# Sampled sequences' cached values in a decoder step: which operand is stationary on TensorE

## What is computed

```
for window, dil in ((128, 1), (512, 4), (2048, 16)):      # three dilation groups
    kg, vg = k_all[:, idx], v_all[:, idx]                  # 128 cached rows each, and the own one
    s = einsum('nqhe,nqjhe->nqhj', q, kg) * 64**-0.5 - slopes * (dil * j)
    p = exp(s - logsumexp(s))
    o = einsum('nqhj,nqjhe->nqhe', p, vg)                  # the values: what is changed
# the three outputs are merged with weights proportional to their softmax denominators
```

## Time and profile before

| | |
|---|---|
| median of 3 runs | 2173.68 us (2171.97 to 2174.41) |
| the profiled execution | 2172.77 us |
| its span, first to last instruction | 2171.1 us |
| granted TensorE clock, mean | 0.984 of full speed |
| TensorE (PE) busy | 2099.8 us, 97% |
| VectorE (DVE) busy | 1175.1 us, 54% |
| ScalarE (ACT) busy | 874.9 us, 40% |
| GpSimd (POOL) busy | 197.5 us, 9% |
| HBM read | 366.86 MB, 171 GB/s over the span |

### The profile page before, as it was taken

How to read it: one execution, slowest core, us unless ns; L and a number is a source line. 1 busy time by engine, 2 the same in 40 slices (tenths; PEclk the granted TensorE clock), 3 DMA queues, 4 the chain that set the end, 5 groups by cost and what they waited for, 6 DMA issues and landing times.

```text
span 2171.1 us, 44928 instructions
## 1 busy us (share of the span) xinstructions
PE 2099.8 (97%) x18500; PEld 2066.8 (95%) x18500; DVE 1175.1 (54%) x1203; ACT 874.9 (40%) x981; POOL 197.5 (9%) x175
## 2 busy tenths in 40 slices
PE   6999999999999999999997879999999999999997
PEld 5999999999999999999995779999999999999997
DVE  5555555555454555669866545555555555544432
ACT  4444444444443443434315424444444444433432
POOL 3000000000000000024202841000000000000000
PEclk9999999999999999999997989999999999999998
DMA  5655555555555566577861025555655555555652
GB/s 160 184 184 176 183 183 178 181 182 181 173 186 177 174 185 196 155 220 227 255 198 39 9 90 175 186 178 183 183 176 182 183 180 179 182 174 186 194 170 93
DMA packets 359390, 373.38 MB, mean 172 GB/s; under 512 B 13397, under 2 KB 351865, under 8 KB 359206
## 3 DMA queue, kind: packets, MB, share of 16 engines
q1 hardware_dynamic: 349280, 348.17, 51.3%
q0 software_dynamic: 6288, 17.51, 3.2%
q10 hardware_dynamic: 3742, 6.52, 0.9%
HBM read 366.86 MB, written 5.32 MB: 171 GB/s over the span
## 4 chain that ended last, share of the span: by engine, by line
PE 93%; DVE 4%; ACT 1%; DMA 1%; issue 1%; ACTq 0%; POOL 0%; POOLq 0%; SPq 0%; DVEq 0%
PE ps L316 29%; PE ps L318 29%; PE ps L317 29%; DVE wL L303 1%; PE ps L1077 1%; PE ps L1418 1%; DMA raw<-in_w_in_dram 1%; DVE xL L350 0%; PE ps L1664 0%; PE ps L1667 0%; PE ps L1675 0%; DMA vrowa<-in_rwkv_mu_dram 0%; PE ps L1706 0%; PE ps L1691 0%; PE ps L1409 0%
## 5 line engine op out<-in xcount | busy, mean ns | idle before, releaser
L303 DVE TENSOR_TENSOR wL<-raw,wH 128x1024 fp32r<-128x1024 f32 (+1 forms) x676 | 828.0, 1231 | 864.5 <-ACT wH L297 864.1
L297 ACT ACTIVATE wH<-raw 128x1024 fp32r<-128x1024 f32 (+1 forms) x676 | 700.0, 1038 | 1013.8 <-PE ps L318 947.8
L316 PE MATMUL ps<-xH,wH 128*128 128x264 f32 x3616 | 1031.7, 285 | 12.3 <-DVE wL L303 12.2
L318 PE MATMUL ps<-xH,wL 128*128 128x264 f32 x3616 | 1029.5, 285 | 0.0
L317 PE MATMUL ps<-xL,wH 128*128 128x264 f32 x3616 | 1029.4, 285 | 0.0
L316 PEld LDWEIGHTS ps<-xH,wH 128*128 128x128 f32 x3616 | 683.6, 189 | 14.2 <-issue 13.4
L318 PEld LDWEIGHTS ps<-xH,wL 128*128 128x128 f32 x3616 | 683.3, 189 | 0.0
L317 PEld LDWEIGHTS ps<-xL,wH 128*128 128x128 f32 x3616 | 682.8, 189 | 0.2
L316 PE MATMUL ps<-hH,wH 128*128 128x264 f32 x1408 | 402.8, 286 | 0.0
L318 PE MATMUL ps<-hH,wL 128*128 128x264 f32 x1408 | 401.9, 285 | 0.0
L317 PE MATMUL ps<-hL,wH 128*128 128x264 f32 x1408 | 401.7, 285 | 0.0
(11 more groups left out here) (355 smaller groups left out, 1131.5 us busy)
## 6 DMA issues: line engine op xcount, KB each, us to landing
raw<-in_ffn_w_gate_dram SPq DMA_DIRECT2D x176, 512.0 KB, 3.5
raw<-in_ffn_w_up_dram SPq DMA_DIRECT2D x176, 512.0 KB, 3.5
raw<-in_ffn_w_down_dram SPq DMA_DIRECT2D x128, 512.0 KB, 3.4
raw<-in_w_in_dram SPq DMA_DIRECT2D x100, 512.0 KB, 4.8
raw<-in_ffn_w_down_dram SPq DMA_DIRECT2D x64, 384.0 KB, 2.9
raw<-in_w_out_dram SPq DMA_DIRECT2D x32, 512.0 KB, 3.6
kb<-in_cache_swa_k_dram POOLq DMA_DIRECT2D x24, 256.0 KB, 6.5
vb<-in_cache_swa_v_dram ACTq DMA_DIRECT2D x24, 256.0 KB, 5.6
```

Source lines behind the costliest of these rows:

```text
L297: nc.scalar.activation(wH[:, k % RING, 0:nk, :], raw[:, k % RING, 0:nk, :], ACT.Copy).then_inc(S("head_made"), 1)
L303: nc.vector.tensor_tensor(wL[:, k % RING, 0:nk, :], raw[:, k % RING, 0:nk, :], wH[:, k % RING, 0:nk, :].bitcast(F32), ALU.subtract).then_i ...
L316: nc.tensor.matmul(out, wH[:, k % RING, q, cols], high, start=a, stop=False)
L318: last = nc.tensor.matmul(out, wL[:, k % RING, q, cols], high, start=False, stop=b)
```

## The change

The roles of the operands are swapped. The probabilities of one sequence and group, 32 columns of `pS` (8 heads, and 24 columns of zeros), are the stationary operand; the 128 x 512 cached values move. The three sequences of a triple write to PSUM partitions 0, 32 and 64, three column groups of 32; the third triple has two sequences. ScalarE copies the bank to `vm`, and TensorE picks for each head pair the rows of its two heads with columns of the identity as the moving operand (`pe_collect_values`), which puts the result back to features on partitions, in bank 5. `pS` is larger and is cleared by POOL. `values_used` now counts triples, and the loads of a triple wait for one signal instead of three.

```diff
-    pS = at("pS", [P, 3, 2, 32], F32, A0 + 37376)
+    pS = at("pS", [P, 3, NB, 32], F32, A0 + 32512)
+    vm = at("vm", [96, 2, 512], F32, A0)
...
-            23: [lambda: act_load_values(act, (3, 4, 5))],
-            24: [lambda: act_load_values(act, (6, 7))],
+            23: [lambda: act_load_values(act, (3, 4, 5)), lambda: act_sample_values(act, 0)],
+            24: [lambda: act_load_values(act, (6, 7)), lambda: act_sample_values(act, 1)],
...
-            22: [lambda: pe_sample_values(pe, (0, 1, 2))],
-            23: [lambda: pe_sample_values(pe, (3, 4, 5))],
-            24: [lambda: pe_sample_values(pe, (6, 7))],
+            22: [lambda: pe_sample_values(pe, 0)],
+            23: [lambda: pe_collect_values(pe, 0), lambda: pe_sample_values(pe, 1)],
+            24: [lambda: pe_collect_values(pe, 1), lambda: pe_sample_values(pe, 2)],
...
                             ).then_inc(S("conv_turned"), 1)
+        pe_collect_values(pe, 2)
...
-    def pe_sample_values(pe, seqs):
-        pe.wait_ge(S("sample_columns"), 1)
-        for b in seqs:
-            pe.wait_ge(S(f"values_in{b % 3}"), 48 * (b // 3 + 1))
-            for j in range(4):
-                m = 4 * b + j
-                for g in range(3):
-                    last = nc.tensor.matmul(
-                        ps[:, 4, 2 * m:2 * m + P].rearrange("p (n a) -> p n a", a=2), vb[:, b % 3, g, j * P:j * P + P],
-                        pS[:, g, :, m].unsqueeze(1).broadcast_to([P, C, 2]), start=g == 0, stop=g == 2)
-            last.then_inc(S("values_used"), 1)
+    TRIPLES = ((0, 1, 2), (3, 4, 5), (6, 7))
+
+    def pe_sample_values(pe, n):
+
+        pe.wait_ge(S("sample_columns"), 2)
+        for b in TRIPLES[n]:
+            pe.wait_ge(S(f"values_in{b % 3}"), 48 * (n + 1))
+        if n:
+            pe.wait_ge(S("values_out"), n)
+        for g in range(3):
+            for b in TRIPLES[n]:
+                rows = slice(b % 3 * 32, b % 3 * 32 + 32)
+                last = nc.tensor.matmul(ps[rows, 4, :], pS[:, g, b, :], vb[:, b % 3, g, :], start=g == 0, stop=g == 2)
+        last.then_inc(S("values_used"), 1)
+
+    def pe_collect_values(pe, n):
+
+        k = len(TRIPLES[n])
+        pe.wait_ge(S("values_out"), n + 1)
+        for j in range(4):
+            pick = ident[0:32 * k, 0:32 * k].rearrange("p (b r) -> p b r", r=32)[:, :, j:j + 5:4]
+            out = ps[:, 5, 64:128].rearrange("p (b j a) -> p b j a", j=4, a=2)[:, 3 * n:3 * n + k, j, :]
+            last = nc.tensor.matmul(out, vm[0:32 * k, n % 2, j * P:j * P + P], pick, start=True, stop=True)
+        last.then_inc(S("values_collected"), 1)
+
+    def act_sample_values(act, n):
+        k = len(TRIPLES[n])
+        act.wait_ge(S("prompt_kv_out"), 32)
+        act.wait_ge(S("values_used"), n + 1)
+        if n == 2:
+            act.wait_ge(S("values_collected"), 1)
+        nc.scalar.activation(vm[0:32 * k, n % 2, :], ps[0:32 * k, 4, :], ACT.Copy).then_inc(S("values_out"), 1)
...
-                act.wait_ge(S("values_used"), b - 2)
+                act.wait_ge(S("values_used"), b // 3)
...
-        act.wait_ge(S("values_used"), NB)
-        act.wait_ge(S("prompt_kv_out"), 32)
+        act.wait_ge(S("values_collected"), 3)
...
-        nc.vector.tensor_copy(pS[:].rearrange("p g a m -> p (g a m)"), ps[:, 7, 0:192]
-                              ).then_inc(S("sample_columns"), 1)
+        dve.wait_ge(S("columns_cleared"), 1)
+        turned = ps[:, 7, 0:192].rearrange("p (g a b j) -> p g a b j", g=3, a=2, j=4)
+        for a in range(2):
+            nc.vector.tensor_copy(pS[:, :, :, 4 * a:4 * a + 4], turned[:, :, a]).then_inc(S("sample_columns"), 1)
...
-        dve.wait_ge(S("values_used"), NB)
+        dve.wait_ge(S("values_collected"), 3)
...
-            v.tensor_tensor(oo[f, :], ps[f, 4, 0:64].rearrange("p (m a) -> p m a", a=2)[:, :, a], osf[f, :], ALU.add
+            v.tensor_tensor(oo[f, :], ps[f, 5, 64:128].rearrange("p (m a) -> p m a", a=2)[:, :, a], osf[f, :], ALU.add
...
+        pool.wait_ge(S("key_products"), NB)
+        nc.gpsimd.memset(pS[:], 0.0).then_inc(S("columns_cleared"), 1)
         for n, a in ((2, 0), (3, 2)):
...
-        pool.wait_ge(S("values_used"), NB)
+        pool.wait_ge(S("values_used"), 3)
...
     def act_gates(act):
+        act_sample_values(act, 2)
         act.wait_ge(S("mixed"), 2)
```

## The result

The changed kernel took 2159.44 us (median of 4 runs, 2157.71 to 2162.93) where the kernel before took 2174.05 us in the same set (4 runs, 2171.97 to 2175.61): the ratio is 0.9939 [0.9925, 0.9953], 14.6 us less. The direction was right. The same kernel was run in two more sets later. Its 15 runs together have a median of 2161.6 us (2157.6 to 2164.4), against 2173.3 us for the 88 runs of the kernel before that stood beside all sets (2169.5 to 2176.6). So the gain is nearer 11.7 us than 14.6, and the first four runs happened to lie low. What follows explains most of both numbers, and says what stays open.

The account below looks back on a forecast made before the run. TensorE bounds the kernel, 93% of the span. Bursts and collections win 10.65 us, the hop gives back 1.15: 9.5 us off 2172.77 is 2163.3, plus 0.9 for the median, 2164.2 us; range 2161.0 to 2168.6.

Parts of the forecast that it names:

- A burst: TensorE's sampled-value matmuls between dense products, stages 22 to 24: about 3.0 us each, where 7.95, 7.95 and 5.35 us stood.
- The change ahead of it I count the same: Switch of matmul shape on TensorE ahead of the value matmuls: taken as 0.2 us, like the switch behind them.
- A collection: TensorE's four matmuls, eight records, that pick each head's rows: 0.9 us, the upper end of 0.5 to 0.9 us.
- The hop: From the third burst's end to L1394, through ScalarE's copy, Tanh, Sigmoid and Square: 4.8 us for 3.66, 1.15 us given back.
- reaction 0.46 us: Delay from the third burst's end to the start of ScalarE's copy, taken from POOL's delay behind the turn.
- Loads of stage 23: Nine value DMAs landing at 1113.9 to 1115.2, wanted by TensorE at 1114.7: slack 0 to 0.5 us, taken as 0.
- The stretch ahead of the first burst: TensorE before stage 22's values: only POOL's memset could cost there, up to 0.5 us over a late weight chunk, taken as 0.
- The width: Forecast's own range, 2161.5 to 2166.5: clock and run spread 1.7 us, collections 0.4 less each, late loads 0.5, POOL 0.5.
- Rival 1: In the three bursts, column groups start in program order: 3.8 us lost, 2168.0 us; chance 0.10.
- Rival 2: Stage 23's cached values land late for the second burst, 4.0 us behind their need: 2168.2 us; chance 0.08.
- Rival 3: In the three bursts, groups don't overlap and each change drains the array: 16.6 us lost, 2180.8 us, slower; chance 0.04.
- Rival 4: Clock fall moving to the front of L1394: 1.1 us lost, or 1.6 us won if it stays up; no chance given.

Follow-up runs that it names:

- e3: Changed kernel with ScalarE's third copy moved behind Tanh and Sigmoid: 2160.72 us, ratio 0.9948 to the kernel before.
- e9: Changed kernel with ScalarE's third copy behind Tanh and Sigmoid and the first nine value loads spread over stages 20 to 22: 2159.26 us, ratio 0.9936.
- e10: e9 with two of VectorE's three rounds of convolution taps moved from stage 21 to stage 22: 2160.24 us, ratio 0.9942 to the kernel before.
- e1: Kernel before with POOL's memset alone, ahead of its stores, and VectorE's wait for it: 2170.68 us, ratio 0.9989.
- e12: Kernel before with the memset alone, placed behind POOL's stores and table loads: 2173.55 us, ratio 0.9999.
- e7: Changed kernel with all sequences of a triple in one column group, values not kept apart: 2175.96 us, ratio 1.0016 to the kernel before.
- e2: Changed kernel with POOL's memset moved behind the loads of the tables: 2164.34 us, ratio 0.9962 to the kernel before.
- e0: Changed kernel run again without any edit: 2161.21 us, ratio 0.9945 to the kernel before.
- e11: Changed kernel run once more without any edit, in another set: 2163.53 us, ratio 0.9949 to the kernel before.
- e5: Kernel before with POOL's three lora table loads moved behind its wait for the turned probabilities: 2172.94 us, ratio 0.9997.
- e13: Kernel before with the memset ahead of the stores and the first nine value loads spread over stages 20 to 22: 2171.91 us, ratio 0.9995.

## Why the prediction was right or wrong

**Direction and main mechanism: right.** The bursts overlap in three column groups. The forecast had 10.65 - 1.15 = 9.5 us for the bursts and the hop; measured are 11.33 - 0.65 = 10.7 us.

- *A burst, 3.0 us expected.* Measured 2.71 us. The 2.60 us of three matmuls in a row are right; the change of shape costs 0.1 us in all, not 0.2 us on each side. The three bursts with their collections beat the forecast by 0.29, 0.31 and 0.11 us. The step "The change ahead of it I count the same" was mis-sized.
- *A collection, 0.9 us expected.* Measured 1112.83 - 1111.95 = 0.88 us, 0.110 us a record. The upper end was the right choice.
- *The hop, +1.15 us expected.* Measured +0.65. Copy (0.59), Tanh to Sigmoid (1131.49 to 1133.64, 2.15 us) and Square (1.51) came as priced. The "reaction 0.46 us" was taken from POOL; ScalarE's copy started 0.16 us behind the turn. That the Square and not `lnwr` or the collection sets L1420's start was right, and e3 shows it.
- *Loads of stage 23, slack 0 to 0.5 us.* No wait in the changed kernel: the landing took 4.7 to 6.3 us, and the burst wanted them at 1112.83. The slack was small, as said. In e9 and e10 the second burst was due as long after the first one (15.3 us), but the loads took up to 8.2 and 8.9 us to land, and TensorE waited 1.7 and 2.6 us.
- *The stretch ahead of the first burst.* This is the step that failed: for it the sum had only POOL's memset, "up to 0.5 us of that could reach TensorE over a late weight chunk, I take 0". The place was right, the size and the sign were not. In the first pair of profiles the late chunk of stage 21 lands 27.2 us behind the start of `pe_values` for 29.4, the wait is 1.0 us for 3.1, and the stretch is 3.5 us shorter. How much of that is the memset's doing stays open. Its 0.74 us (expected near 0.7) stand ahead of the stores and loads. In the kernel before it was worth 2.4 us (e1), and nothing behind the loads (e12). In e7 nothing of a gain is seen, between the changed kernel and e2 the times don't decide, and the wait was 1.0 to 3.4 us with the memset in the same place. So a good part of the 3.5 us was the luck of one execution.
- *The width.* The range counted 1.7 us for "the clock and the spread of runs". One kernel's profiles differ by 3.8 us in the stretch ahead of the first burst alone, and 15 runs by 6.8 us, so a median of four can lie 2 us beside that of fifteen, as it did.

Together: 9.5 us forecast, 1.2 us more from the bursts and the hop, makes 10.7, and this part repeats in every profile of the changed kernel. About 1 us more leads to the 11.7 us of all runs; it may be the memset, but it is no larger than what the runs can't tell apart. 2161.6 us is inside the range. The other 3 us of the first set go with the wait and the clock ahead of stage 22 and with the clock behind L1420, which differ between executions of one kernel. Below 2161.0 us the range had nothing, since POOL's part was only allowed to cost and the spread between executions was put too small.

**The rivals.** Rival 1, a strict order of the column groups, is false: a burst would have taken at least 4.3 us. The Trainium skill (TensorE: Matmul & The Clock Gate, Part 3, The mechanism) has the rule that it came from, that matmuls start and end strictly in program order. The trace does not agree with it for the two records of these matmuls in column groups: the first records of the three groups start 7 ns apart, all within 0.02 us, and the second record of the first matmul only 0.45 us behind its first. Rival 2, late values, is false here and true in e9 and e10. Rival 3, no overlap, is what e7 builds: 2175.96 us, slower than before, as its sign said. The forecast for it, 2180.8 us, had 3.6 us for changes of group, which e7 doesn't make; without them it is 2177.2 us, 1.2 us above e7. Rival 4, the clock, was width, and real: in the first profile the 12 records of L1420 took 4.14 us beside 4.28, in e0 4.52 us, and in e11 5.36 us at a granted clock of 0.52. That is the 5.4 us at half speed that the prediction priced, 1.1 us lost, and it came in one of three profiles of the same kernel.

**Still open.** Whether the memset does anything in the changed kernel, and why a delay of about 0.9 us on POOL's queue should let the chunk of stage 21 land earlier in the kernel before. The value loads compete with it (landing at 25.6 us with them spread, 29.4 without), the tables' loads don't show it in the times (e5), and the stores weren't tried alone. In e13 the stores started 0.3 us behind `pe_values`, no later than the 0.5 to 0.7 us of the kernels without a memset, and 1.6 us in e1; so the memset doesn't always delay them against TensorE. Nor was the wait ahead of stage 22 seen in more than one profile of each experiment, so its mean for each kernel is known only through the times (the unedited kernels have two and three profiles).

## What to carry to other kernels

Small matmuls with few stationary columns belong side by side in column groups, the groups innermost in the order of issue; check in the trace that their first records start together, because in one group the same count was slower than the code replaced. A small instruction on a queue that issues DMAs moves their issue in time: give it a range with a gain in it as well as a loss, as e1 had one. And where a stretch of the trace holds a wait with a half-speed stretch behind it, look at a second profile of the same kernel before putting its length into a sum.

## What the runs showed of the hardware that was not expected

- Three column groups of 32 with all 128 rows and 512 columns ran at 2.9 times the rate of one group, 2.71 us against 7.84 us for nine matmuls. The Trainium skill gives 2.38 for three tiles at 512 columns (TensorE: Matmul & The Clock Gate, Part 3, Measured speedup vs the span model); the trace is nearer to the full three.
- A memset of 0.74 us on POOL, added to the kernel before and used by nobody, went with a faster run: 2170.68 us, 0.9989 [0.998, 0.9998]; behind the table loads it did nothing, 0.9999 [0.999, 1.0008]. The same memset in the changed kernel showed no clear effect.
- One weight chunk landed at 24.2 to 25.9 us in the four profiles with nine value loads spread over three stages, at 27.2 to 29.7 us in the twelve with them together.
- The same program spent 52.65, 54.52 and 56.48 us between the same two instructions in three executions, with a granted clock of 1.00, 0.83 and 0.66 in the 10 us behind one wait of 1.0 to 2.1 us.
